# Attention steps moved one tick apart between engines, output norm's multiply two ticks later, both level factors in one instruction, first two levels on 128 partitions

## The chip, the cores and the metric

The kernel runs on one core of one Trainium2 chip. The metric is the time of one execution in microseconds (us) on the device, as the median of several runs. TensorE is called PE in the rows, its weight loads PEld, VectorE DVE, ScalarE ACT, GpSimd POOL and the queue that issues most transfers SP.

## The reference, cut to what matters

One layer of a hybrid decoder is computed for a prompt of 1024 rows and for 8 sample rows, all in fp32, 1024 features wide. The change touches only what follows the input projection for the prompt:

```python
# sliding-window attention, 8 heads in 2 key groups, blocks of 128 queries, window 128
s = einsum(q, k) * HEAD_DIM ** -0.5            # a block of queries against its own and the block before
m = max(max(s), sink); p = exp(s - m)
a = (p / (sum(p) + exp(sink - m))) @ v
# gated linear recurrence, 4 heads of 128 x 128, f = lb + (1 - lb) * sigmoid(rf), k = 1 - f
S[t] = f[t] * S[t-1] + outer(k[t], i[t]);  o[t] = q[t] @ S[t]
o = o * rsqrt(mean(o * o) + EPS) * rec_norm * silu(rg)
```

The two results are put side by side and go through the output projection; a feed-forward part follows.

## The kernel before, in words

**The mixer is written as ticks.** The input projection has 22 weight tiles (`TILES`) times 3 chunks of 344 rows, which are 66 units. A unit is 24 matmuls of 344 columns (fp32 as high and low parts, three products for each of 8 slices of the features) and takes two ticks of 12 matmuls each. Every engine has a loop over the same 132 ticks, and in each tick it runs the pieces that `attention_steps`, `recurrence_steps`, `sample_steps` and `rot_steps` list for it, in the order of the lists. There is no planner: an engine does its pieces strictly in program order and waits on semaphores for the others. On PE the 12 matmuls of the tick come first and the listed pieces behind them. On DVE the attention pieces come first, then `unit_finish` in even ticks, the recurrence, the sample rows, the low part of a weight tile in every sixth tick, and in odd ticks `unit_read`, which empties the unit's PSUM bank. ACT makes the high part of a weight tile before its attention pieces, and its own `unit_read` comes at the end of an odd tick. Ticks are not synchronised: an engine that is ahead runs on until a semaphore stops it.

**Attention** has 32 items (4 tiles of queries times 8 blocks), one every two ticks from tick 16 (`AT0`). For item i, "Q" splits the queries (ACT high part, DVE low part `q_lo`), "S" is the score matmuls (PE), the copy of their second half out of PSUM (ACT) and mask, maximum and exponent's bias (DVE, four instructions, which end with semaphore `at_max`), "E" the exponentials (ACT) and a difference of values (POOL, `v_diff`), "N" the denominator (DVE), "R" the scaling of the probabilities (ACT), "PT" the transposes (PE), their copy (ACT) and a multiply with a mask into `pt_prev` (DVE), "PV" the product with the values (PE) and its copy into `mix` (ACT). Before the change Q is at tick 16+2i-1, S at 16+2i, E one tick on, N two, R three, PT four and PV six. So in an even tick PE runs PV, PT and S, and DVE's part of S and PT follows ACT's copy of the same tick; in an odd tick ACT runs R, E, Q and DVE's Q follows ACT's Q of the same tick. The scores of all items use one PSUM bank: PE may start S of item i+1 only when DVE has finished its part of S of item i (`at_max`) and when `q_lo` of item i+1 is there (`q_low`).

**The recurrence** of a head h starts at tick 55+18h (`HG0`, `HGS`). One tick earlier, "prep", ACT writes `hk` = 1-f and DVE `hq`; at the tick itself "diag", PE multiplies them; then come seven levels in seven ticks. In level n, PE multiplies `hk` with the later half of the columns of each group of 2*2^n in `hq` into one of two banks. DVE waits for that, then multiplies the later halves of `hq` and the earlier halves of `hk` with factors (`decay`, lines 2081 and 2082), which releases PE's next level (`hq_step`), and then copies the level's product under a mask into `ast` (line 2173). The factors of levels 1 to 6 are made by POOL. Levels 0 to 6 use 127, 126, 124, 120, 112, 96 and 64 partitions. Later steps are two transposes of `hk` (ticks 9 and 10 after the start), the states (11), "o" (13): PE makes the output, ACT squares it and takes a root, which needs another activation table, and DVE waits for that and multiplies (`orn`, which lies on `hk`); "ot" (16): PE transposes the result.

Of the kernel before, what the change touches and what calls it, by code (L numbers as in the profile page):

```python
# [189 lines left out]
def shape_constants():  # L190

    ident = np.eye(P, dtype=np.float32)
    half = ROT // 2
    s, t = np.arange(P)[:, None], np.arange(P)[None, :]
    tri = np.stack([t > s, s > t], axis=1).astype(np.float32)
    lmask = np.stack([(s // (2 * h) == t // (2 * h)) & (s // h % 2 == 0) & (t // h % 2 == 1)
                      for h in (2 ** n for n in range(LEVELS))], axis=1).astype(np.float32)
    pos = np.concatenate([np.arange(SEQ), np.full(DECB, PAST)]).astype(np.float32)
    inv = np.exp(-np.log(np.float32(THETA)) * np.arange(half, dtype=np.float32) * np.float32(2.0 / ROT))
    ang = (pos[None, :] * inv.astype(np.float32)[:, None]).astype(np.float32)  # L200
    cos, sin = np.ones((P, ROWS), np.float32), np.zeros((P, ROWS), np.float32)
    for b in range(0, P, HD):
        for d in range(ROT):
            cos[b + d], sin[b + d] = np.cos(ang[d % half]), np.sin(ang[d % half]) * (-1 if d < half else 1)
    return {"c_ident": ident, "c_tri": tri, "c_lmask": lmask, "c_cos": cos, "c_sin": sin}


def build(nc, t_in, t_out):
# [4 lines left out]
    def at(name, shape, dt, offset):  # L213

        size = math.prod(shape[1:]) * (1 if dt == U8 else 4)
        assert offset + size <= end, (name, offset + size - end)
        return nc.alloc_sbuf_tensor_at(name, shape, dt, offset=offset), (offset + size + 31) // 32 * 32
# [45 lines left out]
    kc_s = small("kc_s", [P, DECB])  # L263
    sinkc = small("sinkc", [DECB * NQ, 1])
    sst = small("sst", [P, 8])
    lmask, o = at("lmask", [P, LEVELS, P], U8, o)
    assert o - small_from <= 4096, o - small_from
    region = small_from + 4096

# [14 lines left out]
    pt_prev, o = at("pt_prev", [P, NKV, P], F32, o)  # L284
    tri, o = at("tri", [P, 2, P], F32, o)
    at_hq = o
    hq, o = at("hq", [P, SEQ], F32, o)
    hk, o = at("hk", [P, SEQ], F32, o)
    at_hg = o
    hg, o = at("hg", [P, 1016], F32, o)  # L290
    ast, o = at("ast", [P, NBLK, P], F32, o)
# [6 lines left out]
    sin, oo = at("sin", [P, ROWS], F32, oo)  # L298
    kwin, oo = at("kwin", [P, P], F32, at_krow - 2 * 4096)
    kn_s, _ = at("kn_s", [DECB, P], F32, oo)  # L300
    lmask32, oo = at("lmask32", [P, LEVELS, P], F32, at_krow - 4096 + 32)
    assert oo <= at_krow
    xr = [at(f"xr{i}", [P, DM], F32, offset)[0] for i, offset in enumerate((at_hq, at_hg, at_hg + 4096))]
    diag, oo = at("diag", [P, RG, P], F32, at_th)
# [262 lines left out]

    def attention_steps(tick):
        d = tick - AT0
        if d % 2 == 0:  # L570
            steps = (("PV", d // 2 - 3), ("PT", d // 2 - 2), ("N", d // 2 - 1), ("S", d // 2))
        else:
            steps = (("R", (d - 3) // 2), ("E", (d - 1) // 2), ("Q", (d + 1) // 2))
        return [(step, i) for step, i in steps if 0 <= i < NITEM]

    def with_prev(i):
# [6 lines left out]
    def recurrence_steps(tick):  # L583

        out = []
        for h in range(NREC):
            d = tick - (HG0 + HGS * h)
            if d in (-4, -1):
                out.append(("it" + "ab"[d == -1], h))
            if d == -1:  # L590
                out.append(("prep", h))
            if d == 0:
                out.append(("diag", h))
            if 1 <= d <= LEVELS:
                out.append(("level", h, d - 1))
            out += [(s, h) for s, v in (("kta", 9), ("ktb", 10), ("u", 11), ("o", 13), ("ot", 16)) if d == v]
        return out

    def gate_input(u):

# [961 lines left out]
    def _(pe):  # L1562
# [42 lines left out]
        for tick in range(TICKS):  # L1605
# [59 lines left out]
            for step in recurrence_steps(tick):  # L1665
# [18 lines left out]
                if step[0] == "level":  # L1684
                    n = step[2]
                    if n:
                        pe.wait_ge(sem("hq_step"), LEVELS * h + n)
                    else:
                        pe.wait_ge(sem("hq_prep"), h + 1)
                    if n == 0:  # L1690
                        take_bl("level_read", LEVELS * (h + 1))
                    elif n >= 2:
                        pe.wait_ge(sem("level_read"), LEVELS * h + n - 1)

                    hs = 1 << n
                    qv = hq[:].rearrange("p (c b e s) -> p c b e s", c=NBLK, e=2, s=hs)
                    for c in range(NBLK):
                        mm = pe.matmul(BL[n % 2][0:P - hs, P // 2 * c:P // 2 * (c + 1)], hk[:, P * c:P * c + P - hs], qv[:, c, :, 1, :],
                                       start=True, stop=True)
                    mm.then_inc(sem("level_mm"), 1)  # L1700
                if step[0] in ("kta", "ktb"):
# [222 lines left out]
    def _(dve):  # L1924
# [146 lines left out]
        def decay(h, n):  # L2071

            hs = 1 << n
            g = r_f[:, 0:SEQ] if n == 0 else g_level(n)
            gv = g.rearrange("p (b e) -> p b e", e=2)
            qv = hq[:].rearrange("p (b e s) -> p b e s", e=2, s=hs)
            kv = hk[:].rearrange("p (b e s) -> p b e s", e=2, s=hs)
            nb = SEQ // (2 * hs)
            if n:
                dve.wait_ge(sem("g_prod"), LEVELS * h + n)  # L2080
            dve.tensor_tensor(qv[:, :, 1, :], qv[:, :, 1, :], bc(gv[:, :, 0].unsqueeze(2), [P, nb, hs]), ALU.mult)
            dve.tensor_tensor(kv[:, :, 0, :], kv[:, :, 0, :], bc(gv[:, :, 1].unsqueeze(2), [P, nb, hs]), ALU.mult)\
                .then_inc(sem("hq_step"), 1)

        def mix_low(i):
            c = BACK[i]
# [5 lines left out]
        for tick in range(TICKS):  # L2092
# [17 lines left out]
            for step, i in attention_steps(tick):  # L2110
                t, j, e = i // NBLK, i % NBLK, i % 2
                k0 = WIN if j == 0 else 0
                if step == "Q":
                    dve.wait_ge(sem("q_high"), i + 1)
                    dve.tensor_tensor(q_lo[:, e, :], mix[:, t, P * j:P * j + P], q_hi[:, e, :].bitcast(F32), ALU.subtract)\
                        .then_inc(sem("q_low"), 1)
                elif step == "S":

                    dve.wait_ge(sem("at_sc"), i + 1)
                    mask = bc(tri[:, 0, :].bitcast(I32).unsqueeze(1), [P, NKV, WIN])  # L2120
                    if j:
                        other = both_groups(BS)[:, :, 0:WIN]
                    else:
                        dve.wait_ge(sem("const_set"), 4)
                        other = bc(neg[:].unsqueeze(1), [P, NKV, WIN])
                    then(dve.copy_predicated(sm[:, e], mask, other))
                    then(dve.tensor_reduce(mx[:, e, :], sm[:, e], AX.X, ALU.max))

                    then(dve.scalar_tensor_tensor(out=negm[:, e, :], in0=mx[:, e, :], scalar=-SCALE, in1=nsink[:, t:t + GRP + 1:GRP],
                                                  op0=ALU.mult, op1=ALU.min))  # L2130
                    dve.tensor_tensor(tsum[:, e, :], sink[:, t:t + GRP + 1:GRP], negm[:, e, :], ALU.add).then_inc(sem("at_max"), 1)
                elif step == "N":

                    dve.wait_ge(sem("at_prob"), 2 * i + 1)
                    then(dve.tensor_tensor(den[:, e, :], den[:, e, :], esk[:, e, :], ALU.add))
                    dve.reciprocal(rden[:, e, :], den[:, e, :]).then_inc(sem("at_den"), 1)
                elif step == "PT" and j:

                    dve.wait_ge(sem("at_ptc"), i + 1)
                    dve.wait_ge(sem("at_pv"), i)  # L2140
                    dve.tensor_tensor(pt_prev[:], pt_all[:], bc(tri[:, 1, :].unsqueeze(1), [P, NKV, P]), ALU.mult)\
                        .then_inc(sem("at_ptp"), 1)
            if tick % 2 == 0 and 0 < tick // 2 <= UNITS - CH:
                unit_finish(tick // 2 - 1)
            for step in recurrence_steps(tick):
# [17 lines left out]
                if step[0] == "level":  # L2163
                    n = step[2]
                    dve.wait_ge(sem("level_mm"), LEVELS * h + n + 1)
                    if n == 0 and h == 0:
                        dve.wait_ge(sem("pool_set"), 4 + CH)
                    decay(h, n)
                    nb, hs = P // (2 << n), 1 << n
                    av = ast[:].rearrange("p c (b e s) -> p c b e s", e=2, s=hs)  # L2170
                    mv = lmask[:, n, :].rearrange("p (b e s) -> p b e s", e=2, s=hs)[:, :, 1, :]
                    k = P - hs
                    dve.copy_predicated(av[0:k, :, :, 1, :], bc(mv[0:k].unsqueeze(1), [k, NBLK, nb, hs]),
                                        BL[n % 2][0:k, :].rearrange("p (c b s) -> p c b s", c=NBLK, s=hs)).then_inc(sem("level_read"), 1)
                    dve.wait_ge(sem("level_read"), LEVELS * h + n + 1)
                if step[0] == "u":
# [5 lines left out]
                    for c in range(NBLK):  # L2182
# [5 lines left out]
                                                           in1=u_c, op0=ALU.mult, op1=ALU.add)  # L2188
                        ins.then_inc(sem("chain"), 1)
                        dve.wait_ge(sem("chain"), NBLK * h + c + 1)  # L2190
                if step[0] == "o":
                    dve.wait_ge(sem("o_std"), h + 1)
                    then(dve.reciprocal(orstd[:], ostd[:]))

# [441 lines left out]
```

## Time and profile before

| | us |
|---|---|
| median of 3 runs | 1235.0 (1232.33 to 1240.39) |
| the profiled execution | 1236.13 |
| its span, first to last instruction | 1234.3 |
| PE busy | 1197.9 (97%) |
| DVE busy | 883.8 (72%) |
| ACT busy | 515.9 (42%) |
| mean granted clock of TensorE | 0.988 of full |

The mixer's ticks fill the span from 9.9 us, where the first unit's matmul starts, to 447.6 us; output projection and feed-forward part follow. A wait in the rows is idle time of an engine just before an instruction, with the instruction that released it; where the profile shows no releaser it is called "issue". The two levels of the clock are 1.2 and 2.4 GHz, in the rows 0.50 and 1.00.

### The profile page before, as it was taken

To read this page: it belongs to the slowest core of one execution; us is meant where nothing else is said; L and a number is where in the kernel's file an instruction comes from. 1 tells how busy PE (TensorE), PEld (TensorE's weight loads), DVE (VectorE), ACT (ScalarE), POOL (GpSimd) and SP (SyncE) were. 2 spreads that over 40 slices of the span, in tenths; PEclk is the share of its full clock that TensorE was granted. 3 is DMA by queue.
4 is the path that set the end of the run, shared out by engine and by line. 5 is a ranking of instruction groups with operands and counts; after the bars stand their busy time and mean duration, and the time that the engine had idled before them with its cause. 6 is when DMAs were issued, how large, how long until landed. Compare 5 with 4: busy or idle time off the path is not lost.

```text
span 1234.3 us, 23340 instructions
## 1 busy us (share of the span) xinstructions
PE 1197.9 (97%) x9189; PEld 1175.8 (95%) x9189; DVE 883.8 (72%) x1458; ACT 515.9 (42%) x1125; POOL 241.4 (20%) x190
## 2 busy tenths in 40 slices
PE   9899989999999999999999999999999999999997
PEld 9899989889998999998999999999999999999996
DVE  4877556574657685789877788887788576567676
ACT  6665654734232274445422232232222235455542
POOL 1000010100101000000032246557564220000011
PEclk9899989999999999999999999999999999999998
DMA  9431100102656433234344466676765366676466
GB/s 297 112 91 35 35 18 2 38 18 62 62 70 85 124 113 128 70 87 137 86 146 146 149 204 234 206 260 201 256 227 190 129 208 216 199 260 185 143 154 118
DMA packets 174012, 169.79 MB, mean 138 GB/s; under 512 B 23144, under 2 KB 126328, under 8 KB 173376
## 3 DMA queue, kind: packets, MB, share of 16 engines
q1 hardware_dynamic: 171728, 164.78, 45.8%
q0 software_dynamic: 2176, 3.52, 1.8%
q8 instruction: 73, 1.20, 0.4%
q14 instruction: 35, 0.29, 0.1%
HBM read 116.73 MB, written 52.58 MB: 137 GB/s over the span
## 4 chain that ended last, share of the span: by engine, by line
PE 58%; DVE 6%; issue 2%; ACT 1%; DMA 0%; DVEq 0%; SPq 0%; ACTq 0%
PE pair L1826 31%; PE pair L1866 18%; PE pair L1785 6%; PE pair L1569 3%; DVE mix L2312 1%; DVE w_lo L2270 1%; ACT w_hi L1113 1%; DVE mix L2337 0%; DMA raw<-w_up_dram 0%; DVE qinv L2308 0%; PE pair L1768 0%; DVE act_lo L2320 0%; PE pair L1757 0%; DVE mix L2475 0%; DVE u_tmp L2415 0%
## 5 line engine op out<-in xcount | busy, mean ns | idle before, releaser
L1826 PE MATMUL pair<-act_hi,w_hi 128*128 128x258 f32 x704 | 199.6, 284 | 4.5 <-DVE w_lo L2270 3.0
L1826 PE MATMUL pair<-act_hi,w_lo 128*128 128x258 f32 x704 | 198.9, 282 | 0.0
L1826 PE MATMUL pair<-act_lo,w_hi 128*128 128x258 f32 x704 | 198.7, 282 | 0.0
L1866 PE MATMUL pair<-a_ring,w_hi 128*128 128x258 f32 x1056 | 189.6, 282 | 0.6 <-DVE mix L2475 0.4
L1569 PE MATMUL pair<-act_hi,w_hi 128*128 128x344 f32 x528 | 178.5, 338 | 0.4 <-DVE w_lo L1939 0.4
L1569 PE MATMUL pair<-act_hi,w_lo 128*128 128x344 f32 x528 | 172.0, 326 | 0.0
L1569 PE MATMUL pair<-act_lo,w_hi 128*128 128x344 f32 x528 | 171.8, 325 | 0.0
L1866 PEld LDWEIGHTS pair<-a_ring,w_hi 128*128 128x128 f32 x1056 | 162.5, 189 | 1.6 <-DVE mix L2475 0.9
L1113 ACT ACTIVATE w_hi<-rawx 128x512 fp32r<-128x512 f32 (+3 forms) x100 | 69.6, 696 | 196.7 <-PE pair L1826 79.7
L1826 PE MATMUL pair<-s_hi,w_hi 128*128 128x258 f32 x528 | 149.5, 283 | 0.5 <-DVE w_lo L2270 0.5
L1826 PE MATMUL pair<-s_hi,w_lo 128*128 128x258 f32 x528 | 149.3, 283 | 0.0
L1826 PE MATMUL pair<-mix_r,w_hi 128*128 128x258 f32 x528 | 149.0, 282 | 0.0
L1866 PE MATMUL pair<-a_ring,w_lo 128*128 128x258 f32 x528 | 148.2, 281 | 0.0
L1826 PEld LDWEIGHTS pair<-act_hi,w_hi 128*128 128x128 f32 x704 | 133.1, 189 | 5.3 <-DVE w_lo L2270 3.4
L1826 PEld LDWEIGHTS pair<-act_lo,w_hi 128*128 128x128 f32 x704 | 132.8, 189 | 0.1
L1826 PEld LDWEIGHTS pair<-act_hi,w_lo 128*128 128x128 f32 x704 | 132.7, 188 | 0.0
L1569 PEld LDWEIGHTS pair<-act_hi,w_hi 128*128 128x128 f32 x528 | 102.5, 194 | 2.1 <-DVE w_lo L1939 0.7
L1569 PEld LDWEIGHTS pair<-act_lo,w_hi 128*128 128x128 f32 x528 | 102.4, 194 | 0.8
L1569 PEld LDWEIGHTS pair<-act_hi,w_lo 128*128 128x128 f32 x528 | 101.9, 193 | 0.0
L1826 PEld LDWEIGHTS pair<-s_hi,w_hi 128*128 128x128 f32 x528 | 99.7, 189 | 1.1 <-DVE w_lo L2270 1.1
L1866 PEld LDWEIGHTS pair<-a_ring,w_lo 128*128 128x128 f32 x528 | 99.9, 189 | 0.0
L1826 PEld LDWEIGHTS pair<-mix_r,w_hi 128*128 128x128 f32 x528 | 99.9, 189 | 0.0
(328 smaller groups left out, 2657.0 us busy)
## 6 DMA issues: line engine op xcount, KB each, us to landing
raw<-w_up_dram SPq DMA_DIRECT2D x26, 512.0 KB, 5.2
a_in<-h_sums SPq DMA_DIRECT2D x44, 258.0 KB, 3.1
rawx<-w_gate_dram SPq DMA_DIRECT2D x22, 512.0 KB, 4.8
w_quarter<-w_down_dram SPq DMA_DIRECT2D x44, 256.0 KB, 4.1
w_sums<-w_quarter SPq DMA_DIRECT2D x44, 256.0 KB, 4.5
rawx<-w_sums SPq DMA_DIRECT2D x44, 256.0 KB, 4.1
raw<-w_in_dram SPq DMA_DIRECT2D x18, 512.0 KB, 4.7
h_scratch<-mix SPq DMA_DIRECT2D x23, 258.0 KB, 2.2
```

The costliest lines, as they stand in the source:

```text
L1113: return act.activation(out, in_, ACT.Copy)
L1569: mm = pe.matmul(out, a[:, k, :], b[:, k, cols(c)], start=(k == 0 and s == 0), stop=(k == KT - 1 and s == 2))
L1785: mm = pe.matmul(bank[(slot + 2) % 4][:, 0:QW], a[:, k, :], b[:, k, quad(slot // NOUT)], start=(k == 0 and s == 0), stop=(k == KT - 1 and ...
L1826: mm = pe.matmul(pair[psum_pair(n)][:, s, 0:QW], a[:, r, half + k, :], b, start=(k == 0 and i == 0), stop=(k == 3 and i == 2))
L1866: mm = pe.matmul(dpair(mt)[:, s, 0:a.shape[1]], b[:, cut], a, start=(m == 0 and n == 0), stop=(m == HALVES - 1 and n == 2))
L2270: dve.tensor_tensor(w_lo[:, r, 0:k], src, w_hi[:, r, 0:k].bitcast(F32), ALU.subtract).then_inc(sem("wf_split"), 1)
L2312: ins = dve.scalar_tensor_tensor(out=x, in0=x, scalar=gain[:, PRE_FFN, k:k + 1], in1=qinv[:], op0=ALU.mult, op1=ALU.mult)
```

## The change

- `attention_steps` is rewritten. For item i: Q at 16+2i-2, S (PE and ACT) at 16+2i, DVE's part of S as a step of its own, "D", at 16+2i+1, E at +2, N at +3, R at +4, PT (PE, ACT) at +5, DVE's multiply of PT as a step of its own, "M", at +6, PV at +7. ACT's even ticks are now Q, R, E, S and its odd ticks PV, PT; PE's even ticks have S, its odd ticks PV, PT; DVE's even ticks M, Q and its odd ticks N, D.
- DVE's part of "o" goes two ticks later, as a step "on" at 15.
- `hq` and `hk` become two halves of one tile `hqk`, and the two multiplies of `decay` become one with a pattern over both.
- Levels 0 and 1 use 128 partitions in the matmul and the masked copy; the mask holds only the columns that are used, now side by side.

```diff
-    lmask = np.stack([(s // (2 * h) == t // (2 * h)) & (s // h % 2 == 0) & (t // h % 2 == 1)
-                      for h in (2 ** n for n in range(LEVELS))], axis=1).astype(np.float32)
+    late = [t[:, t[0] // h % 2 == 1] for h in (2 ** n for n in range(LEVELS))]
+    lmask = np.stack([(s // (2 << n) == t // (2 << n)) & (s >> n & 1 == 0) for n, t in enumerate(late)], axis=1).astype(np.float32)
...
-    hq, o = at("hq", [P, SEQ], F32, o)
-    hk, o = at("hk", [P, SEQ], F32, o)
+    hqk, o = at("hqk", [P, 2 * SEQ], F32, o)
+    hq, hk = hqk[:, 0:SEQ], hqk[:, SEQ:2 * SEQ]
...
     def attention_steps(tick):
         d = tick - AT0
+        a = d // 2
         if d % 2 == 0:
-            steps = (("PV", d // 2 - 3), ("PT", d // 2 - 2), ("N", d // 2 - 1), ("S", d // 2))
+            steps = (("M", a - 3), ("Q", a + 1), ("R", a - 2), ("E", a - 1), ("S", a))
         else:
-            steps = (("R", (d - 3) // 2), ("E", (d - 1) // 2), ("Q", (d + 1) // 2))
+            steps = (("PV", a - 3), ("PT", a - 2), ("N", a - 1), ("D", a))
...
-            out += [(s, h) for s, v in (("kta", 9), ("ktb", 10), ("u", 11), ("o", 13), ("ot", 16)) if d == v]
+            out += [(s, h) for s, v in (("kta", 9), ("ktb", 10), ("u", 11), ("o", 13), ("on", 15), ("ot", 16)) if d == v]
+    def level_keys(n):
+        return P if n < 2 else P - (1 << n)
...  (PE, level)
-                        mm = pe.matmul(BL[n % 2][0:P - hs, P // 2 * c:P // 2 * (c + 1)], hk[:, P * c:P * c + P - hs], qv[:, c, :, 1, :],
+                        mm = pe.matmul(BL[n % 2][0:k, P // 2 * c:P // 2 * (c + 1)], hk[:, P * c:P * c + k], qv[:, c, :, 1, :],
...  (DVE, decay)
-            dve.tensor_tensor(qv[:, :, 1, :], qv[:, :, 1, :], bc(gv[:, :, 0].unsqueeze(2), [P, nb, hs]), ALU.mult)
-            dve.tensor_tensor(kv[:, :, 0, :], kv[:, :, 0, :], bc(gv[:, :, 1].unsqueeze(2), [P, nb, hs]), ALU.mult)\
-                .then_inc(sem("hq_step"), 1)
+            late_q_early_k = hqk[:, hs:2 * SEQ - hs].rearrange("p (w m s) -> p w m s", w=2, s=hs)[:, :, 0::2, :]
+            factors = bc(g.rearrange("p (b w) -> p w b", w=2).unsqueeze(3), [P, 2, nb, hs])
+            dve.tensor_tensor(late_q_early_k, late_q_early_k, factors, ALU.mult).then_inc(sem("hq_step"), 1)
...  (DVE, the steps)
-                elif step == "S":
+                elif step == "D":
...
-                elif step == "PT" and j:
+                elif step == "M" and j:
...
-                    mv = lmask[:, n, :].rearrange("p (b e s) -> p b e s", e=2, s=hs)[:, :, 1, :]
-                    k = P - hs
+                    mv = lmask[:, n, :].rearrange("p (b s) -> p b s", s=hs)
+                    k = level_keys(n)
...
-                if step[0] == "o":
+                if step[0] == "on":
                     dve.wait_ge(sem("o_std"), h + 1)
```

## Rows read from the trace of the kernel before

**Rows 1.** The page, parts 1 and 2: busy us, and the clock granted in 40 slices.
```profile
PE 1197.9 (97%) x9189; PEld 1175.8 (95%) x9189; DVE 883.8 (72%) x1458; ACT 515.9 (42%) x1125; POOL 241.4 (20%) x190
PEclk9899989999999999999999999999999999999998
```
**Rows 2.** Waits of PE in 0 to 620 us: total us, times, longest.
```profile
PE pair L1698 <- DVE hk L2082: 7.9, 7, 2.3
PE pair L1644 <- issue: 6.8, 7, 2.4
...
PE pair L1681 <- ACT hk L1198: 1.5, 2, 1.2
```
**Rows 3.** PE in order of time: start, us, instruction, idle before it.
```profile
47.19 0.55 PE L1644 MATMUL pair<-k_hi,q_hi 128*128 128x256 f32 x1 [2.78 <-DVE q_lo L2115]
...
56.03 0.47 PE L1644 MATMUL pair<-k_hi,q_hi 128*128 128x512 f32 x1 [1.81 <-issue]
...
233.94 0.47 PE L1644 MATMUL pair<-k_hi,q_hi 128*128 128x512 f32 x1 [2.42 <-issue]
...
255.77 1.97 PE L1698 MATMUL pair<-hq,hk 128*126 128x64 f32 x16 [1.46 <-DVE hk L2082]
...
402.02 1.57 PE L1698 MATMUL pair<-hq,hk 128*96 128x64 f32 x16 [2.32 <-DVE hk L2082]
```
**Rows 4.** Waits of PE in 60 to 165 us.
```profile
PE pair L1644 <- issue: 2.6, 5, 0.7
```
**Rows 5.** Waits of PE in 170 to 280 us.
```profile
PE pair L1698 <- DVE hk L2082: 4.9, 5, 1.5
```
**Rows 6.** Waits of PE in 300 to 412 us.
```profile
PE pair L1698 <- DVE hk L2082: 3.0, 2, 2.3
```
**Rows 7.** Stretches: length, busy us (instructions) of PE, PEld, DVE, ACT, POOL, granted clock, DMA.
```profile
50.00:53.40 3.40, 3.40 (x24) 3.24 (x24) 1.99 (x6) 1.21 (x3) 0.27 (x1) 1.00 0.00 0
56.80:60.20 3.40, 3.40 (x13) 3.39 (x12) 2.38 (x9) 2.69 (x8) 0.00 (x0) 0.50 0.00 0
176.30:183.10 6.80, 6.80 (x27) 6.53 (x26) 3.60 (x6) 0.49 (x1) 0.00 (x0) 0.50 0.00 0
...
333.30:336.70 3.40, 3.40 (x16) 3.40 (x14) 2.28 (x7) 1.44 (x2) 0.00 (x0) 0.50 0.16 43
...
300.00:320.00 20.00, 20.00 (x151) 19.95 (x150) 8.04 (x15) 12.28 (x34) 4.04 (x7) 1.00 0.71 67
...
80.00:100.00 20.00, 19.37 (x119) 18.39 (x118) 15.67 (x55) 10.88 (x40) 1.64 (x3) 1.00 0.40 129
```
**Rows 8.** Groups of DVE by form in 0 to 620 us: busy, mean ns, idle before.
```profile
L1939 DVE TENSOR_TENSOR w_lo<-raw,w_hi 128x1024 fp32r<-128x1024 f32 x26 | 31.8, 1221 | 7.8 <-ACT w_hi L1113 7.5
L2081 DVE TENSOR_TENSOR hq<-hq,hg 128x512 f32<-128x512 f32 x24 | 18.9, 786 | 15.5 <-PE pair L1698 7.8 <-issue 7.6
L2082 DVE TENSOR_TENSOR hk<-hk,hg 128x512 f32<-128x512 f32 x24 | 16.4, 684 | 0.0
L2127 DVE TENSOR_REDUCE mx<-sm 128x2 f32<-128x256 f32 x32 | 13.4, 420 | 1.1
...
L2141 DVE TENSOR_TENSOR pt_prev<-pt_all,tri 128x256 f32<-128x256 f32 x28 | 12.4, 442 | 31.8 <-ACT pt_all L1113 31.6
...
L2151 DVE TENSOR_TENSOR hq<-r_q,r_f 128x1024 f32<-128x1024 f32 x4 | 4.9, 1234 | 4.5 <-ACT f_s L1113 4.5
...
L2173 DVE COPY_PREDICATED ast<-lmask,pair 127x512 f32<-127x512 uint8 x4 | 5.2, 1297 | 0.0
...
L2173 DVE COPY_PREDICATED ast<-lmask,pair 124x512 f32<-124x512 uint8 x4 | 2.8, 698 | 0.0
```
**Rows 9.** Waits of DVE in 215 to 450 us.
```profile
DVE orstd L2193 <- ACT ostd L1132: 23.5, 4, 7.4
```
**Rows 10.** Groups of ACT by form in 60 to 300 us.
```profile
L1288 ACT ACTIVATE prob<-prob,rden 128x128 f32<-128x128 f32 x62 | 21.4, 394 | 12.9 <-DVE rden L2136 12.9
...
L1132 ACT ACT_TABLE_LOAD x1 | 1.3, 1283 | 0.0
```

More of the change, by code:

```diff
@@ L265, in build @@
     sst = small("sst", [P, 8])
-    lmask, o = at("lmask", [P, LEVELS, P], U8, o)
+    lmask, o = at("lmask", [P, LEVELS, P // 2], U8, o)
     assert o - small_from <= 4096, o - small_from
@@ L300, in build @@
     kn_s, _ = at("kn_s", [DECB, P], F32, oo)
-    lmask32, oo = at("lmask32", [P, LEVELS, P], F32, at_krow - 4096 + 32)
+    lmask32, oo = at("lmask32", [P, LEVELS, P // 2], F32, at_krow - 4096 + 32)
     assert oo <= at_krow
@@ L2074, in decay @@
             g = r_f[:, 0:SEQ] if n == 0 else g_level(n)
-            gv = g.rearrange("p (b e) -> p b e", e=2)
-            qv = hq[:].rearrange("p (b e s) -> p b e s", e=2, s=hs)
-            kv = hk[:].rearrange("p (b e s) -> p b e s", e=2, s=hs)
             nb = SEQ // (2 * hs)
+            late_q_early_k = hqk[:, hs:2 * SEQ - hs].rearrange("p (w m s) -> p w m s", w=2, s=hs)[:, :, 0::2, :]
+            factors = bc(g.rearrange("p (b w) -> p w b", w=2).unsqueeze(3), [P, 2, nb, hs])
             if n:
                 dve.wait_ge(sem("g_prod"), LEVELS * h + n)
-            dve.tensor_tensor(qv[:, :, 1, :], qv[:, :, 1, :], bc(gv[:, :, 0].unsqueeze(2), [P, nb, hs]), ALU.mult)
-            dve.tensor_tensor(kv[:, :, 0, :], kv[:, :, 0, :], bc(gv[:, :, 1].unsqueeze(2), [P, nb, hs]), ALU.mult)\
-                .then_inc(sem("hq_step"), 1)
+            dve.tensor_tensor(late_q_early_k, late_q_early_k, factors, ALU.mult).then_inc(sem("hq_step"), 1)
         def mix_low(i):
@@ L2170, in _ @@
                     av = ast[:].rearrange("p c (b e s) -> p c b e s", e=2, s=hs)
-                    mv = lmask[:, n, :].rearrange("p (b e s) -> p b e s", e=2, s=hs)[:, :, 1, :]
-                    k = P - hs
+                    mv = lmask[:, n, :].rearrange("p (b s) -> p b s", s=hs)
+                    k = level_keys(n)
                     dve.copy_predicated(av[0:k, :, :, 1, :], bc(mv[0:k].unsqueeze(1), [k, NBLK, nb, hs]),
```

## The prediction

> **What bounds the kernel now.** The page first: PE is busy 97% of the span, DVE 72%, ACT 42% [rows 1]. So only PE's idle time and its slow clock can be won; the change takes nothing off PE. The waits of PE say how much: in the first 620 us it sits idle before a level's matmul for 7.9 us, before the scores of an attention item for 6.8 us, before "diag" for 1.5 us [rows 2] and once 2.8 us for `q_lo` [rows 3], about 19 us in all and all inside the ticks the change rewrites. In order of time they are a few stops of 1.5 to 2.8 us and many of half a microsecond [rows 3]. The granted clock comes next: it falls to half (1.2 GHz) behind several stops. A slow stretch of 3.4 us holds 13 PE instructions where the full clock ran 24 [rows 7], and 11 matmuls at the full pitch (20 us for 151 of them in a busy stretch, [rows 7], is 0.13 to 0.16 us each) are 1.6 us lost. The one of 6.8 us has 27 where 51 would fit at that rate, 3.2 us lost.
>
> Then why DVE is late though it has time: it waits 31.8 us for ACT's copy of the same tick before the `pt_prev` multiply [rows 8] and 23.5 us, four times, for ACT's root in "o" [rows 9]. In an even tick DVE gets to `decay` only behind that copy, the denominator, the mask, the maximum (0.42 us) and `unit_finish`, while PE, with no attention in the next odd tick, is back after 12 matmuls.
>
> **Part by part**, against the profiled execution's 1236.1 us.
>
> *Levels beside attention (heads 0 and 1).* DVE's even tick keeps the multiply with the mask (M, 0.44 us [rows 8]), whose copy was made a tick before, and Q. The denominator and the mask part move to the odd tick, where their inputs are a tick old and PE has PV and PT before its level (about 1.1 us, estimated from starts in order of time, like the other times of PE's attention pieces below). `decay` then starts when the level's matmuls end and needs 1.2 us, against 1.9 us of PE's next 12 matmuls. The five waits of 4.9 us [rows 5] go, and I give back the slow stretch of 6.8 us behind the first, 3.2 us: **8.1**.
> What does the row say on the clock? It fell at 176.3 [rows 7] behind a stop at this head's levels, and did not fall behind one of 1.46 us at 255.8 [rows 3]; at 333.3 it fell with no wait listed before it [rows 7], behind matmuls of few columns. So a filled gap need not bring the clock back; without this 3.2 the sum is that much smaller, and that end goes into the range. The Trainium skill, "TensorE: Matmul & The Clock Gate", Part 1, has half clock as the default that activity releases; by that every stretch behind a filled gap comes back, 3.2 here, and the one at 333.3 would not be expected, which the trace contradicts.
>
> *Scores in plain ticks.* `q_lo` came from ACT's Q at the end of the same odd tick; now it is made two ticks ahead. In its place S of item i+1 waits for D of item i, one tick before. That chain is S on PE 0.8, ACT's copy 0.4, D 1.3 us (mask, 0.42 for the maximum, two small ones), 2.5 us, plus what ACT has ahead of its copy; between two S, PE has 24 matmuls, PV and PT, 4.9 us. It fits. The five waits, 2.6 us [rows 4], go: **2.6**.
>
> *Start.* The 2.78 us at 47.2 [rows 3] stay: Q of item 0 stands behind the same DVE work, tick 13's unit, as before. The 1.81 at 56.0 becomes about 0.6: `q_lo` is early, but D of item 0 now follows DVE's `row_angles` of tick 17. 1.2, and the slow stretch behind it [rows 7] 1.6: **2.8**.
>
> *"diag".* 1.2 of its 1.5 us [rows 2] is head 0. ACT's even tick before "prep" grows: Q, R, E, S, with R and E four passes of about 0.39 us (R's in [rows 10]) and small ones, about 0.9 more than before; but its odd tick shrinks by as much, DVE reads the gate's unit about 2.5 us earlier (not behind `q_lo`), and PE has PV and PT before "diag". I get `hk` some 0.4 us before PE. Head 3's 0.3 goes with DVE's earlier read: **1.5**.
>
> *The output norm.* DVE no longer stands 5.9 us (23.5 by 4, [rows 9]). With attention running this happens for head 0 alone, and it caused the 2.42 at 233.9 [rows 3] and a slow stretch, 1.6. What is late next is ACT: eight squares, a table load of 1.28 [rows 10], the root and a second load are the same, with the attention copies behind them. DVE's Q at tick 70 waits for ACT's before "on", and `hk` of head 1 comes behind E and S. I put 0.2 at "ot" and 1.1 at "diag" against it: **2.7**. For heads 1 to 3 nothing on PE waited, so 0.
>
> *Longer or later levels (heads 2 and 3).* Merging: 0.79+0.68 by the means, or twice 0.68 undisturbed, against 1.23 for 1024 elements [rows 8]; with the overlap of neighbours only 0.1 is saved each. The pattern over two halves is not in the trace: between 1.23 (the row) and 2.5 (two inputs at the 2.4 ns per element of the 127-partition copy). I take 1.23, since 512 elements at any stride cost 0.68 already. Masked copy: 1.30 at 127 and 126 partitions, 0.70 at 124 [rows 8]; partitions or the spread-out mask, both go; between 0.7 and 1.3, I take 0.7. These 0.6 fill about 1.2 of the 3.0 us in [rows 6] and small ones. The 2.32 at 402.0 stays, with the clock behind it: there the sample rows' eight multiply-adds and the gate stand between two levels. **1.3**.
>
> *Nothing for:* one or two columns more in eight levels on PE (at most 0.01 us a matmul, 1 us in all if not hidden), POOL's difference one tick later (PV comes five ticks behind), and SP, which waits at tick 85 for `at_out` one tick longer, with the sample caches needed three ticks on.
>
> Sum 8.1+2.6+2.8+1.5+2.7+1.3 = 19.0. 1236.1-19.0 = 1217.1; the median shown is 1.1 below that execution, which makes 1216. I add 1 for small waits not foreseen: **1217**. If all waits within reach went, with their stretches: 21, so 1214; the least, with no clock back (6.4), 1223.
>
> **Rivals.**
> (a) *The clock does not come back*, or falls elsewhere beside the short matmuls, as at 333.3. 19.0-6.4 = 12.6: 1222 to 1223.
> (b) *ACT becomes late.* Its four attention steps now stand in one tick ahead of "prep" and of PE's PT. For it: R and E already wait for nobody but DVE, and the root with two table loads fills over a tick. Against: 42% busy. If head 0's and 1's "diag", "ot" and some PT each wait 1 to 2 us with one more slow stretch, 8 to 9 come off the gain: 1226.
> (c) *Slower: `at_max` becomes the bound.* The S, copy, D chain has 1.2 us of slack over ACT's 2 us of Q, R, E ahead of the copy (4.9-2.5 = 2.4, less what ACT cannot do ahead). If DVE enters the odd tick more than that behind, because a rotary unit's four instructions (about 2) and a weight's low part (1.22, [rows 8]) stand before, PE waits at each S: at 1.1 us in 31 items 34 us, less 19: 1250. It decides when D ends after PE's second 12 matmuls; DVE's 15.7 busy in 20 us of those ticks [rows 7] speaks against it, 0.8 of the time being in use with 1.2 a pair of ticks to spare.
> (d) *The merged multiply or the 128-partition copy is no faster*, at the upper bounds: `decay` of 2.5 against 1.9 us leaves 0.6 before about 14 levels with no attention between, 8 us: 1225.
>
> **Chances.** Forecast 0.54, (a) 0.17, (b) 0.13, (c) 0.07, (d) 0.09. A change under 1%, 12 us, cannot be told from none; that line is at 1223. The forecast is faster nearly whole (0.53), of (a) 0.10; of (b) and (d) none; slower by 1% is (c). Faster 0.63, same 0.30, slower 0.07. Range: forecast and (a) span 1212 to 1223; to leave out no more than 2 in 10 it reaches through (b) and (d): 1212 to 1229.
>
> **What would show it.** Right: no wait of PE behind `hk` between 170 and 280 us, the scores' waits below 1 us outside the start, no wait of DVE for `ostd`, 28 multiplies of 1.23 us, copies of 0.7 at 128 partitions, mean clock above 0.99, and still a stop of 2.8 before item 0 and one near 2.2 in head 3's levels. Wrong: waits of PE for ACT's `hk` or `prob`, or scores waiting for `tsum`.

## The result and the profile after

The changed kernel takes **1217.87 us** (median of 4 runs, 1215.41 to 1220.45) against 1234.82 (4 runs, 1232.33 to 1240.39) for the kernel before: a ratio of 0.9857, 95% interval 0.9816 to 0.9897. The profiled execution took 1219.23 us with a span of 1217.4 and a mean clock of 0.991. The ratios here and below are worked out from all runs of a kernel and differ a little from quotients of the medians. The forecast was 1217, range 1212 to 1229. PE's first output-projection matmul starts at 432.3 us, where it was 447.8, so in the profiled executions 15.5 of the 16.9 us come from the mixer's ticks and 1.4 from what follows.

The page first, parts 1 and 2, as in [rows 1].
```profile
PE 1192.0 (98%) x9189; PEld 1173.9 (96%) x9189; DVE 887.7 (73%) x1430; ACT 512.7 (42%) x1125; POOL 245.0 (20%) x190
PEclk9999999999998999999999999999999999999999
```
PE's idle time, span less busy, fell from 36.4 to 25.4 us and its busy time by 5.9. The waits of PE in the first 450 us say which idle time went; they answer to [rows 2, 4 to 6].
```profile
PE pair L1735 <- DVE hqk L2200: 4.2, 2, 3.2
PE pair L1704 <- DVE hqk L2086: 3.1, 3, 2.2
PE pair L1649 <- DVE q_lo L2118: 1.6, 1, 1.6
...
PE pair L1649 <- DVE tsum L2134: 0.7, 1, 0.7
PE pair L1656 <- ACT prob L1293: 0.3, 1, 0.3
```
L1735 is the transposes of "ot", L1704 a level, L1649 the scores (a wait of 1.1 at the very start, for `neg`, the same in every kernel here, is left out). Now PE in order of time, as in [rows 3]: these are all its waits of 0.3 us or more between 40 and 450 us.
```profile
45.81 0.36 PE L1649 MATMUL pair<-k_hi,q_hi 128*128 128x256 f32 x1 [1.62 <-DVE q_lo L2118]
...
52.31 0.47 PE L1649 MATMUL pair<-k_hi,q_hi 128*128 128x512 f32 x1 [0.69 <-DVE tsum L2134]
...
217.79 0.44 PE L1656 MATMUL pair<-ident,prob 128*128 128x128 f32 x2 [0.30 <-ACT prob L1293]
...
219.18 1.09 PE L1735 MATMUL pair<-ident,hqk 128*128 128x128 f32 x8 [0.94 <-DVE hqk L2200]
...
302.75 1.95 PE L1704 MATMUL pair<-hqk 128*124 128x64 f32 x16 [0.54 <-DVE hqk L2086]
...
369.19 1.89 PE L1704 MATMUL pair<-hqk 128*120 128x64 f32 x16 [0.34 <-DVE hqk L2086]
...
378.69 2.67 PE L1704 MATMUL pair<-hqk 128*96 128x64 f32 x16 [2.20 <-DVE hqk L2086]
...
418.10 1.09 PE L1735 MATMUL pair<-ident,hqk 128*128 128x128 f32 x8 [3.24 <-DVE hqk L2200]
```
Read against [rows 4, 5]: no wait at the scores or a level between 60 and 280 us, where eleven made 9.9: the ten of [rows 4, 5], 7.5, and the 2.42 at 233.9. And one stop is new, the longest: 3.24 at 418.1, before the last head's transposes. The named waits add up to 9.9 us where they were 19.4, which is the 19.0 of [rows 2, 3] and 0.47 before a level at 392.4 for which the view names no releaser.

Stretches of the clock, columns as in [rows 7]: the three at half clock in the mixer, and the place where 6.8 us ran at half before.
```profile
310.60:314.00 3.40, 3.40 (x16) 3.40 (x14) 2.80 (x4) 1.44 (x2) 1.90 (x1) 0.50 0.64 34
378.90:389.10 10.20, 10.20 (x52) 9.83 (x52) 4.96 (x8) 0.49 (x1) 0.00 (x0) 0.50 0.38 103
419.90:423.30 3.40, 3.40 (x13) 3.40 (x13) 2.58 (x5) 1.60 (x3) 0.00 (x0) 0.50 0.44 127
176.00:182.80 6.80, 6.80 (x56) 6.50 (x55) 5.28 (x14) 4.82 (x17) 0.46 (x1) 1.00 0.00 1
```
The clock granted was half in 17.0 us of the mixer, against 23.8 before in six places. At the rate of [rows 7], 13 instructions where 24 ran, the 6.8 us less are worth 3.1. With 9.5 of named waits that is 12.6 of the mixer's 15.5; the other 2.9 are in waits and in distances between starts too small to be put to a place.

Groups of DVE by form in 0 to 620 us, as in [rows 8].
```profile
L2086 DVE TENSOR_TENSOR hqk<-hqk,hg 128x1024 f32<-128x1024 f32 x24 | 30.5, 1270 | 16.2 <-PE pair L1704 8.3 <-issue 7.8
...
L2176 DVE COPY_PREDICATED ast<-lmask,pair 128x512 f32<-128x512 uint8 x8 | 10.4, 1302 | 0.0
...
L2086 DVE TENSOR_TENSOR hqk<-hqk,r_f 128x1024 f32<-128x1024 f32 x4 | 4.9, 1222 | 0.3 <-PE pair L1704 0.3
...
```
The merged multiply costs about what was taken (1.23), 1.22 to 1.27 us. DVE's wait for ACT's copy of `pt_all`, in the same view, fell from 31.8 to 6.5. The masked copy on 128 partitions is **not** 0.7 us: 1.302.

**The new stop** is seen when DVE and ACT are read in order of time ahead of 418.1. DVE:
```profile
413.53 0.15 DVE L2246 RECIPROCAL sst<-sst 32x1 f32<-32x1 f32 x1 [6.33 <-ACT sst L1137]
...
415.33 0.52 DVE L2070 SCALAR_TENSOR_TENSOR th<-th,r_f 128x344 f32<-128x344 f32 x1 [0.85 <-ACT th L1216]
...
416.32 0.20 DVE L2196 RECIPROCAL orstd<-ostd 128x8 f32<-128x8 f32 x1
...
416.75 1.29 DVE L2200 TENSOR_TENSOR hqk<-pair,orstd 128x512 f32<-128x512 f32 x2
```
and ACT:
```profile
411.32 1.28 ACT L1137 ACT_TABLE_LOAD   x1
412.62 0.30 ACT L1137 ACTIVATE ostd<-oss,eps 128x8 f32<-128x8 f32 x1
...
413.20 0.29 ACT L1137 ACTIVATE sst<-sst,eps 32x1 f32<-32x1 f32 x1
413.51 1.28 ACT L1216 ACT_TABLE_LOAD   x1
414.81 0.49 ACT L1216 ACTIVATE th<-r_f 128x344 f32<-128x344 f32 x1
```
The root of "o" (`ostd`) is ready at 412.9, yet its multiply ends at 418.0. DVE no longer stands at `ostd`; it stands 6.33 us at the sample rows' root (`sst`), whose ACT work is queued behind the same squares and the same table load, and then 0.85 at the gate's tanh behind the second load. Only then does it come to "on". Before, the same place read like this (DVE, then PE):
```profile
433.31 0.20 DVE L2193 RECIPROCAL orstd<-ostd 128x8 f32<-128x8 f32 x1 [5.75 <-ACT ostd L1132]
433.55 0.17 DVE L2195 TENSOR_SCALAR orstd<-orstd 128x8 f32<-128x8 f32 x1
433.76 1.29 DVE L2197 TENSOR_TENSOR hk<-pair,orstd 128x512 f32<-128x512 f32 x2
```
```profile
435.10 1.09 PE L1729 MATMUL pair<-ident,hk 128*128 128x128 f32 x8
```
DVE stood 5.75 us and was done in time; PE did not wait at all.

### The profile page after: what moved, and what is told of

The parts are those of the page before. It is cut to its first block, busy times and chain, and to the rows that moved or that the text cites. A ratio compares the mean times of both kernels' runs of the same rounds, so it can differ in the third digit from the quotient of the medians.

```text
span 1217.4 us, 23314 instructions
## 1 busy us (share of the span) xinstructions
PE 1192.0 (98%) x9189; PEld 1173.9 (96%) x9189; DVE 887.7 (73%) x1430; ACT 512.7 (42%) x1125; POOL 245.0 (20%) x190
## 4 chain that ended last, share of the span: by engine, by line
PE 62%; DVE 5%; issue 1%; ACT 1%; DVEq 0%; ACTq 0%
PE pair L1832 33%; PE pair L1872 18%; PE pair L1791 6%; PE pair L1574 2%; DVE mix L2315 1%; DVE mix L2340 1%; DVE w_lo L2273 1%; DVE qinv L2311 1%; PE pair L1763 0%; PE pair L1704 0%; PE pair L1774 0%; DVE act_lo L2323 0%; DVE mix L2478 0%; DVE acc L2377 0%; DVE mix L2298 0%
```

## The experiments

The theory: the gain is nearly all the attention steps' (on record for experiment 1: about 14 us), and the output norm's step at 15 costs what the two edits on the levels may give. Its rival: each part gives what its term said (15.0 and 4.0). Twelve kernels ran, in four series; the kernel before had medians of 1233.8, 1235.42, 1234.82 and 1234.07 in them, and ratios are against the one of the same series.

**1. The attention steps alone** (the kernel before with these lines).
```diff
-            steps = (("PV", d // 2 - 3), ("PT", d // 2 - 2), ("N", d // 2 - 1), ("S", d // 2))
+            steps = (("M", a - 3), ("Q", a + 1), ("R", a - 2), ("E", a - 1), ("S", a))
         else:
-            steps = (("R", (d - 3) // 2), ("E", (d - 1) // 2), ("Q", (d + 1) // 2))
+            steps = (("PV", a - 3), ("PT", a - 2), ("N", a - 1), ("D", a))
```


> The kernel before with the new attention steps alone; norm's multiply at 13, two multiplies per level, 127 and 126 partitions as before. Theory (DVE's even ticks were too full of work that waited for ACT in the same tick): the five waits of PE at the levels beside attention (4.9 us), the five small ones before the scores (2.6 us) and head 0's before 'diag' (1.2 us) are gone, with the slow-clock stretches at about 57 and 176 us; PE still waits about 2 us for the scores near 230 us, behind DVE's wait for the root. Time about 14 us below before, near 1221. Rival (the shorter DVE work of the merged multiply and the wider copy carries the gain at the levels): the waits at the levels stay above 2.5 us in sum, and the time is 4 to 6 us below before, near 1230.

Measured: 1216.97 (1214.83 to 1218.94), ratio 0.9863 (0.9841 to 0.9884), clock 0.995. That is 16.8 us, the whole gain and more than the 14 expected. The profiled execution, the fastest of the five, is 21.3 us shorter than that of the kernel before: its waits are 9.5 us where they were 19.4, and its clock was half for 6.8 us of the mixer where it was for 23.8, which is 9.9 and, at the rate above, 7.8 of them. Waits of PE in 0 to 450 us:
```profile
PE pair L1699 <- DVE hk L2083: 4.5, 4, 2.3
PE pair L1645 <- DVE tsum L2132: 2.7, 2, 2.0
PE pair L1645 <- DVE q_lo L2116: 2.0, 1, 2.0
...
```
The levels' 4.5 us all lie beyond 290 us. The 2.0 before the scores for `tsum` is at 217.1, where DVE still stood at head 0's root: with the new steps too, the norm at 13 makes PE wait for head 0.

**2. All but the attention steps** (the changed kernel with the old lists of steps).
```diff
-            steps = (("M", a - 3), ("Q", a + 1), ("R", a - 2), ("E", a - 1), ("S", a))
+            steps = (("PV", d // 2 - 3), ("PT", d // 2 - 2), ("N", d // 2 - 1), ("S", d // 2))
         else:
-            steps = (("PV", a - 3), ("PT", a - 2), ("N", a - 1), ("D", a))
+            steps = (("R", (d - 3) // 2), ("E", (d - 1) // 2), ("Q", (d + 1) // 2))
```


> The changed kernel with the old attention steps: merged multiply, 128 partitions and the norm's multiply at 15 stay. Theory: waits at the levels beside attention stay near 4.5 us and those before the scores near 3 us; only the 2.4 us stop near 234 us and some of the late ones go, and the new 3.2 us stop at the last head's transposes comes. Time 0 to 4 us below before, 1231 to 1235. Rival: 10 us or more below before, near 1224.

Measured: 1239.77 (1236.69 to 1243.33, 8 runs), ratio 1.0046 (1.0026 to 1.0066): slower than before. Neither theory had foreseen that. PE around head 0's "ot":
```profile
227.96 0.47 PE L1648 MATMUL pair<-k_hi,q_hi 128*128 128x512 f32 x1 [2.42 <-issue]
...
233.97 1.97 PE L1734 MATMUL pair<-ident,hqk 128*128 128x128 f32 x8 [3.19 <-DVE hqk L2199]
```
The stop at the scores that the norm's move was to remove is there unchanged (2.42, now for `q_lo`, which waits 7.14 us for ACT behind the root's table loads: the view names no releaser for PE, but `q_lo` ends 0.1 us before it), and a second of 3.19 has come at the transposes; the last head has one of 3.2 too. The wait of DVE for ACT does not go with the multiply: something else in its queue stands there in its place.

**3. The norm at 14 instead of 15**, all else as changed, and **4. the changed kernel again**, on the same chip.
```diff
-            out += [(s, h) for s, v in (("kta", 9), ("ktb", 10), ("u", 11), ("o", 13), ("on", 15), ("ot", 16)) if d == v]
+            out += [(s, h) for s, v in (("kta", 9), ("ktb", 10), ("u", 11), ("o", 13), ("on", 14), ("ot", 16)) if d == v]
```


> The changed kernel with DVE's norm multiply at tick 14 of a head, not 15, so that for the last head it stands ahead of the sample rows' wait for their root and of a gate read. Theory: PE's 3.24 us stop before the last head's transposes goes (DVE then waits about 6 us for the root but releases PE at once), with the slow stretch behind it, and the 0.9 us of head 0 too; 4 to 5 us below the changed kernel, near 1213, clock 0.995. Rival (ACT's root, not DVE's order, sets that stop): the stop stays above 2 us, and DVE's longer wait in tick 69 brings back a wait before the scores near 220 us: 1218 or above.

> The changed kernel itself, as the measure for the others of this series: 1218 us, within 2 us, about 17 below before. Both theories expect the same; if the slow-clock stretches at 300 and 379 us are chance, at least one of them is elsewhere or gone in this profile.

Measured: at 14, 1213.69 (1210.78 to 1217.54), ratio 0.9846 (0.9821 to 0.9871); at 15, 1220.42 (1219.09 to 1221.8), ratio 0.9891 (0.987 to 0.9912), with the stops of 0.94 and 3.23 at "ot" again. No run is in common, and by the medians the step at 15 costs 6.7 us against 14. In the profiled executions the stops at "ot", less the waits that 14 has in their place, are 3.4 of it and the half clock behind the second 1.6; the rest lies at places where waits and half clock move between executions of one kernel. The other pair of series, the changed kernel's first (0.9857) and experiment 5 below (0.984), has the same sign but is only 2 us apart, with intervals that overlap; so the size is 2 to 7 us. In this series the changed kernel is also 3.4 us slower than the attention steps alone (experiment 1); its first ratio is 0.7 us better than theirs. So the other three parts together lose a few us or give nothing, where the sum had 4.0 of gain; the rival falls. DVE and PE of the last head, norm at 14:
```profile
408.68 0.20 DVE L2196 RECIPROCAL orstd<-ostd 128x8 f32<-128x8 f32 x1 [5.75 <-ACT ostd L1137]
...
409.12 1.29 DVE L2200 TENSOR_TENSOR hqk<-pair,orstd 128x512 f32<-128x512 f32 x2
```
```profile
410.46 1.09 PE L1735 MATMUL pair<-ident,hqk 128*128 128x128 f32 x8
```
DVE stands at the root for as long as in the kernel before, and PE waits for none of it. At head 0 the stop at "ot" is gone too; 0.50 before "diag" and 0.3 for `prob` are what is left of ACT's lateness.

These two executions also show how much the last two heads' waits vary from one execution to another. The 2.20 of head 3 is 0.65 in experiment 3 and 0.66 in 4, and the wait at 369 us is 1.01 and 1.24 where it was 0.34. DVE's gate instruction ahead of it ran beside one of POOL and took 1.20 and 1.43 us instead of 0.52 (last section), which is the growth of the wait; the clock then fell there, at 370.3 and 374.3, and PE came to the next level later, so its stop was shorter.

**5 to 8. What is the rest worth, with the norm at 14?** 5 repeats experiment 3. 6 is the attention steps and the norm at 14 with neither edit on the levels. 7 has two multiplies in place of one:
```diff
-            dve.tensor_tensor(late_q_early_k, late_q_early_k, factors, ALU.mult).then_inc(sem("hq_step"), 1)
+            dve.tensor_tensor(qv[:, :, 1, :], qv[:, :, 1, :], bc(gv[:, :, 0].unsqueeze(2), [P, nb, hs]), ALU.mult)
+            dve.tensor_tensor(kv[:, :, 0, :], kv[:, :, 0, :], bc(gv[:, :, 1].unsqueeze(2), [P, nb, hs]), ALU.mult)\
+                .then_inc(sem("hq_step"), 1)
```
8 moves `unit_finish` on DVE behind the recurrence of its tick:
```diff
-            if tick % 2 == 0 and 0 < tick // 2 <= UNITS - CH:
-                unit_finish(tick // 2 - 1)
             for step in recurrence_steps(tick):
...
+            if tick % 2 == 0 and 0 < tick // 2 <= UNITS - CH:
+                unit_finish(tick // 2 - 1)
             for step in sample_steps(tick):
```


> The norm's multiply at 14 as before, the measure for the other three of this series: 1214 us within 2, about 20 below before.

> The kernel before with the new attention steps and the norm's multiply at 14, but two multiplies per level and 127 and 126 partitions. Theory (merged multiply and 128 partitions bring next to nothing): within 2 us of norm-at-14, waits at the levels of the last two heads 1 to 1.5 us larger. Rival (they were the part that lost against attention alone): 3 us or more below norm-at-14, at 1211. Second rival (they bring what I had put on them, 1.3 us and more): 2 us or more above it, at 1216.

> Norm-at-14 with the merged multiply written as two again (0.69 us each), 128 partitions kept. Theory: within 1.5 us of norm-at-14, since two in a row took 1.29 us from start to end and the one takes 1.22; PE's waits at the levels 0.1 us longer each where they are. Rival (one long instruction is held up longer by GpSimd's work on the shared memory side, or holds it up): faster than norm-at-14 by 2 us or more.

> Norm-at-14 with DVE's unit_finish (the gate's multiply, which waits for ACT's tanh) put behind the recurrence's pieces of the same tick. Theory (in the last head's levels PE waits because unit_finish and its wait stand before the factors): the waits at the levels fall from 2.2 us to under 0.8 us, slow stretches near 380 us go with them, time 2 to 4 us below norm-at-14, near 1211. Rival (the eight multiply-adds for the sample rows alone set it): waits stay above 1.5 us, time the same.

| | us | ratio | level waits beyond 290 us |
|---|---|---|---|
| 5 | 1215.34 (1214.62 to 1218.7) | 0.984 (0.9815 to 0.9865) | 3.1, longest 2.2 |
| 6 | 1217.37 (1215.3 to 1218.33) | 0.9847 (0.9823 to 0.9871) | 3.5, longest 2.3 |
| 7 | 1216.57 (1214.53 to 1219.49) | 0.9843 (0.9817 to 0.9868) | 4.2, longest 2.3 |
| 8 | 1210.76 (1209.45 to 1214.57) | 0.9801 (0.9778 to 0.9825) | 0.9, longest 0.6 |

The runs of 5, 6 and 7 lie over each other: with these steps, what merging and the 128 partitions are worth (0 to 2 us) is not told apart from nothing. Nor is the norm at 14 (experiment 6, 0.9847) told apart from the norm at 13 (experiment 1, 0.9863) with the new attention steps. 8 is below 5 with no run in common, though barely (1214.57 against 1214.62), and 5 to 6 us below experiments 3 and 5 by the ratios. Why is in DVE's rows at head 3. The changed kernel, ahead of PE's stop at 378.69:
```profile
373.07 2.19 DVE L2236 SCALAR_TENSOR_TENSOR st<-ib,k_s,st 128x128 f32<-128x128 f32 x8
...
376.24 0.52 DVE L2070 SCALAR_TENSOR_TENSOR th<-th,r_i 128x344 f32<-128x344 f32 x1 [0.56 <-ACT th L1216]
...
377.42 1.22 DVE L2086 TENSOR_TENSOR hqk<-hqk,hg 128x1024 f32<-128x1024 f32 x1
```
and experiment 8:
```profile
372.79 2.19 DVE L2236 SCALAR_TENSOR_TENSOR st<-ib,k_s,st 128x128 f32<-128x128 f32 x8
...
375.32 1.22 DVE L2086 TENSOR_TENSOR hqk<-hqk,hg 128x1024 f32<-128x1024 f32 x1
```
The sample rows' 2.19 us stay, but the gate (its wait for ACT's tanh and three instructions) no longer stands before the factors, which start 1.8 us earlier behind the same work. The stop shrinks from 2.2 to 0.3, and the half clock behind it from 10.2 us (in 5 too) to 3.4. The levels' waits are 2.1 us less and the 6.8 us less at half clock are 3.1, together about what 8 is below 5; against experiment 3, which had no stop of 2.2, only the runs' times show the gain.

**9. The sample rows' root one tick later.** If DVE's 6.33 us at `sst` is what makes "on" late, this takes it from before "on".
```diff
-        out += [(s,) for s, v in (("r_rows", 0), ("r_cols", 2)) if d == v]
+        out += [(s,) for s, v in (("r_rows", 1), ("r_cols", 3)) if d == v]
```


> The changed kernel (norm's multiply at 15) with only the sample rows' last norm moved: r_rows one tick later, tick 124 instead of 123, r_cols likewise one tick later, so that DVE's wait for that root stands behind the last head's norm multiply. Theory (the 3.24 us stop is DVE's order: the 6.3 us wait in r_rows, then a gate read and its multiply, stand ahead of the norm's multiply): the stop falls from 3.2 to under 1 us, head 0's 0.9 stays; 3 to 5 us below the changed kernel, near 1215 to 1217. Rival (ACT's root and table load set it): the stop stays at 3.

Measured: 1217.41 (1216.73 to 1220.93), ratio 0.9863 (0.9843 to 0.9883); the stop is 2.65 at 417.05, hardly less. The expectation failed. DVE's rows:
```profile
414.29 0.52 DVE L2070 SCALAR_TENSOR_TENSOR th<-th,r_f 128x344 f32<-128x344 f32 x1 [3.23 <-ACT th L1216]
...
415.27 0.19 DVE L2196 RECIPROCAL orstd<-ostd 128x8 f32<-128x8 f32 x1
```
With `sst` out of the way DVE stands at the gate instead, since that tanh comes behind ACT's root and both table loads. Either wait suffices to make "on" late.

**10. The old attention steps and the norm at 13, with the two edits on the levels** (experiment 2 with `("on", 13)`).

> The kernel before with the merged multiply and 128 partitions only (old attention steps, norm's multiply at 13). Theory (these two are worth little, and the loss of the kernel with all but attention came from the norm's place): 0 to 2 us below before, no stop at the heads' last transposes, the waits at the levels 4 to 5 us beside attention as before. Rival (the merged multiply or the wide copy costs time by itself): 3 us or more above before.

Measured: 1230.86 (1229.74 to 1235.31), ratio 0.9973 (0.9951 to 0.9995). So merging and 128 partitions give 0.6 to 6 us by the interval, 3.3 by the ratio, in the old schedule, where 0 to 2 was expected. Against experiment 2 (1.0046, another series) only the norm's tick differs: at 15 it costs 0.73%, 9 us, of which the two new stops at "ot" are 6.4.

**11. What makes the masked copy slow** (norm at 14): at levels 0 and 1 the copy writes its columns side by side, so these two levels' products are left out of their places in `ast`.
```diff
-                    dve.copy_predicated(av[0:k, :, :, 1, :], bc(mv[0:k].unsqueeze(1), [k, NBLK, nb, hs]),
+                    late_cols = ast[0:k, :, 0:P // 2].rearrange("p c (b s) -> p c b s", s=hs) if n < 2 else av[0:k, :, :, 1, :]
+                    dve.copy_predicated(late_cols, bc(mv[0:k].unsqueeze(1), [k, NBLK, nb, hs]),
```


> Norm-at-14, but the masked copy of levels 0 and 1 writes its columns side by side into the first half of each block, not to every second column or pair; what the levels bring to the recurrence's output is thereby left wrong. Theory (neither the partitions nor the mask made 1.30 us, since 128 partitions and the packed mask take it too; the output's runs of one or two elements do): 0.70 us at levels 0 and 1, as at the others. Rival (the short runs of PSUM reads or the level itself): 1.30 stays.

Measured (one run): 1212.85. The copy:
```profile
L2177 DVE COPY_PREDICATED ast<-lmask,pair 128x512 f32<-128x512 uint8 x8 | 5.8, 728 | 0.0
```
0.728 us instead of 1.302, on the same 128 partitions with the same mask. It is where the copy writes, runs of one or two elements with as many left out, and neither partitions nor mask.

**12. The norm at 15 with `unit_finish` behind the recurrence** (the edit of 8 on the changed kernel). By experiment 9 the gate is the last thing between `sst` and "on".

> The changed kernel, norm's multiply at 15 and the sample rows' norm in its place, with only unit_finish put behind the recurrence's pieces of the same tick. After the miss of rows-later, two things stand ahead of the norm's multiply, one behind the other: the wait for the sample rows' root, and the gate's multiply, which waits for a tanh behind ACT's two table loads. Theory (both count): PE's 3.2 us stop falls to about 1.3 us, what the first leaves (DVE is free at 414.0, reads a unit to 414.5 and needs 1.7 us for the norm; PE came at 414.9), and head 3's 2.2 us stop at the levels to under 0.8; time about 1213, 2 us above the same with the norm's multiply at 14. Rival (the gate's multiply alone made it): the stop falls under 0.5 us and the time is 1211. Second rival (the place of the gate doesn't matter): stop 2.7 or more, 1218.

Measured: 1211.94 (1210.44 to 1213.62, 6 runs), ratio 0.9823 (0.9796 to 0.9851). PE, then DVE:
```profile
412.98 1.09 PE L1735 MATMUL pair<-ident,hqk 128*128 128x128 f32 x8 [1.31 <-DVE hqk L2198]
```
```profile
410.34 0.15 DVE L2246 RECIPROCAL sst<-sst 32x1 f32<-32x1 f32 x1 [5.77 <-ACT sst L1137]
...
411.22 0.18 DVE L2194 RECIPROCAL orstd<-ostd 128x8 f32<-128x8 f32 x1
```
The stop fell by 1.9, to 1.31, which is what `sst` alone leaves. With experiment 9 this closes the account of the 3.24: the sample rows' root alone makes 1.31, the gate alone 2.65, and each hides part of the other. Experiments 8 and 12, the norm at 14 and at 15 with the gate behind, are not told apart (0.9801 and 0.9823, intervals that overlap); 8 is some 7 us below the changed kernel by the ratios 0.9801 and 0.9857.

## Why the forecast was right, and where its steps were not

The time was right, 1217 against 1217.87, but as a sum in which errors cancel: that it came out to 1 us is luck. What was right in mechanism is the attention steps' part, 15.0 of the 19.0.

*Levels beside attention, 8.1: right.* The five waits of [rows 5] are gone, and 176.0 to 182.8 runs 56 instructions at full clock where 27 ran. On the question that the row left open, the clock came back behind this gap in every kernel with the new steps; so the first half of rival (a) did not happen. Its second half, a fall elsewhere beside the short matmuls, did in part: 17.0 us at half clock are left where the forecast's terms left 10.2. What "TensorE: Matmul & The Clock Gate" of the Trainium skill gives (3.2 us back) agrees with it here. But the stretch at 310.6 us has no wait of 0.1 us or more in the 7 us before it: it lies behind 16 matmuls of 64 columns and 16 of 8, as did that at 333.3 before. Filling gaps did not do away with those; in the kernels with the new steps they begin between 305 and 315 and between 370 and 386 us, now none, now one or several.

*Scores in plain ticks, 2.6: right*, all gone; in the changed kernel rival (c) shows itself only as the 0.69 at 52.3.

*Start, 2.8: right for what it named.* 1.81 became 0.69, as worked out (0.6). The 2.78 was to stay and fell to 1.62, and the half-clock stretch behind it was gone in this execution. Neither is shown to be the change's: the wait is 1.2 to 2.6 in the twelve others, 1.8 and 2.05 in the two with the old attention steps, and the stretch is there in experiments 4, 6, 9 and 10.

*"diag", 1.5: right*, and the 1.1 put against the norm at head 1's "diag" did not come with the norm at 15; at 14 it is 0.5. Of rival (b) that, the 0.3 for `prob` and 0.9 at "ot" are all.

Together these attention terms were 15.0, and experiment 1 measured 16.8.

*The output norm, 2.7: wrong, and the step of the forecast that failed, though the time did not show it.* It said "For heads 1 to 3 nothing on PE waited, so 0". That priced what the move removes (nothing) and left out what the moved instruction lands behind, which the forecast had done for head 0 alone. At head 3 the multiply now stands behind the sample rows' root and the gate's tanh: 3.24 us and a half-clock stretch of 3.4 us behind it (in experiment 4 too), 1.6 more. At head 0 it is 2.42 and 1.6 won and 1.24 lost where 0.2 was set. In place of 2.7: 4.0 less 1.2 less 4.8, about 2 lost. Experiment 3 shows that DVE's 23.5 us of waiting [rows 9] were no loss to PE except at head 0: with the norm at 14 DVE still waits 20.3 us for `ostd` beyond 215 us, and that kernel is 2 to 7 us faster. (Of "no wait of DVE for `ostd`", a sign of being right, the changed kernel keeps 2.8 us in two waits there.)

*Later levels, 1.3: wrong in one of its two terms.* The merged multiply is 1.22 to 1.27 us, the low bound taken; rival (d)'s price for it did not occur. The masked copy was taken at 0.7 between bounds of 0.7 and 1.3 and is 1.302: the forecast had "partitions or the spread-out mask, both go", and the cause is a third, the spread-out output (experiment 11), which did not go. The levels' waits beyond 290 us are 3.1 against 3.5, which is the 3.0 of [rows 6] and the 0.47 at 392.4: 0.4 won. The 2.32 that was to stay, stayed, at 2.20, but the half clock behind it grew from 3.4 to 10.2 us in this execution (two stretches of 3.4 in experiment 4's), 3.2 lost.

So the failed terms are short of the sum of 19.0 by 4.8 (norm) and 0.9 and 3.2 (later levels), 8.9 in all. Against them stand the start (1.2 of waits, 1.6 of clock), the 2.9 in small ones and 1.4 behind the mixer, 7.1: 17.2, where 16.9 was measured, and 18.0 forecast with the allowance of 1. These 7.1, which the forecast did not have, are not shown to be the change's: the median moves by 2.5 us between two series of the same changed kernel.

## What to carry to other kernels

When engines run one list of steps in order, let each step consume what another engine made a tick earlier; that paid 16.8 us here with no work removed, since the waits on the engine that is the bound came from same-tick hand-offs. A wait of an engine that is not the bound costs only through what is queued behind it, so before a step is moved away from such a wait, read what stands in front of its new place and what that waits for: here two ticks later cost 2 to 7 us against one, and one against none is not told apart. Of an instruction that is slow in one form, change one property at a time (partitions, mask, output runs) before the fix is priced.

## What the runs showed of the hardware

- A masked copy of 512 fp32 elements out of PSUM takes 1.30 us when its output runs are one or two elements long and 0.70 to 0.73 when they are four or longer or side by side. DVE's multiply does not care: 1222 ns for 1024 elements at level 0, where both input and output go in single elements, the same as for a plain one [rows 8].
- A DVE instruction with both inputs in SBUF that starts beside a long one on POOL is held up. In the changed kernel, DVE and POOL:
```profile
312.07 2.18 DVE L2063 SCALAR_TENSOR_TENSOR r_q<-th,r_q 128x344 f32<-128x344 f32 x1 [0.56 <-issue]
```
```profile
311.98 1.90 POOL L1050 TENSOR_TENSOR st<-st,f_s 128x1024 f32<-128x1024 f32 x1 [19.81 <-DMA st<-state_hgrn_dram]
```
The same instruction takes 0.51 to 0.52 us at its other places, and 2.18 ends just behind POOL's. In experiment 4 it set a wait of PE, the 1.24 named under experiments 3 and 4:
```profile
368.85 1.43 DVE L2070 SCALAR_TENSOR_TENSOR th<-th,r_i 128x344 f32<-128x344 f32 x1 [0.56 <-ACT th L1216]
```
```profile
368.01 1.90 POOL L1050 TENSOR_TENSOR st<-st,f_s 128x1024 f32<-128x1024 f32 x1 [10.82 <-DMA st<-state_hgrn_dram]
```
An instruction with one input in PSUM is not held up: in the changed kernel `r_i<-pair,r` at 365.86 takes 0.52 us beside POOL's 2.39 from 363.97. "SBUF — State Buffer", "SBUF: two separate sides", of the Trainium skill describes an exclusive lock on a shared port pair for a DVE instruction with two SBUF inputs against one of POOL that reads SBUF; the rows agree.
